# A fused two-block transformer kernel: weight chunks taken later in the delta rule, the last square of each norm summed on TensorE, and a Newton step that needs no square from ScalarE

## What is computed

```
def rms_norm(x, gain):
    xf = x.astype(jnp.float32)
    y = xf * lax.rsqrt(jnp.mean(xf * xf, axis=-1, keepdims=True) + EPS)
    return (y * gain.astype(jnp.float32)).astype(x.dtype)
...
    """Chunked gated delta rule.
    S_t = exp(g_t) (I - beta_t k_t k_t^T) S_{t-1} + beta_t k_t v_t^T,  o_t = S_t^T q_t.
    q, k: [B,H,S,dk] (L2-normed), v: [B,H,S,dv], beta, g: [B,H,S]; float32."""
```

## Time and profile before

| | |
|---|---|
| median of 3 runs | 3218.89 us (3216.57 to 3220.13) |
| profiled execution, its own time | 3218.03 us |
| its span | 3216.2 us |
| granted TensorE clock, mean | 0.955 |
| TensorE busy | 2951.7 us |
| VectorE, ScalarE, GpSimd busy | 1562.7, 1074.6, 195.0 us |

### The profile page before, as it was taken

How to read it: one execution, slowest core, us unless ns; L and a number is a source line. 1 busy time by engine, 2 the same in 40 slices (tenths; PEclk the granted TensorE clock), 3 DMA queues, 4 the chain that set the end, 5 groups by cost and what they waited for, 6 DMA issues and landing times.

```text
span 3216.2 us, 47860 instructions
## 1 busy us (share of the span) xinstructions
PE 2951.7 (92%) x21522; PEld 2380.4 (74%) x21522; DVE 1562.7 (49%) x2201; ACT 1074.6 (33%) x1408; POOL 195.0 (6%) x157
## 2 busy tenths in 40 slices
PE   4999999789999989999799899789999896889999
PEld 3877888567788868888566666578888684578887
DVE  6666554464577643232555555543333655443332
ACT  3225233343233235243422322232222656432221
POOL 1010000201222110001000000010000000000000
PEclk9999999899999989999889888799999998999999
DMA  7554453121000022222110110022323220122321
GB/s 270 183 183 157 183 183 141 53 79 40 16 3 3 17 105 96 101 92 98 56 53 29 39 40 27 14 90 77 115 84 101 77 74 1 51 80 72 118 88 63
DMA packets 41724, 269.66 MB, mean 84 GB/s; under 512 B 4272, under 2 KB 4528, under 8 KB 13488
## 3 DMA queue, kind: packets, MB, share of 16 engines
q1 hardware_dynamic: 39648, 260.86, 22.8%
q10 hardware_dynamic: 1872, 5.74, 0.5%
HBM read 264.49 MB, written 2.10 MB: 83 GB/s over the span
## 4 chain that ended last, share of the span: by engine, by line
PE 81%; DVE 9%; ACT 6%; issue 3%; DMA 1%; POOL 1%; SPq 0%; POOLq 0%; DVEq 0%; ACTq 0%
PE ps L637 19%; PE ps L638 19%; PE ps L643 19%; PE ps L2000 4%; PE ps L2739 1%; PE ps L1578 1%; PE ps L1561 1%; PE ps L1572 1%; PE ps L2058 1%; DVE WL L409 1%; PE ps L2089 1%; DMA W<-w_ada 1%; ACT WH L401 1%; DVE qk L2264 1%; DVE TMP L602 1%
## 5 line engine op out<-in xcount | busy, mean ns | idle before, releaser
L637 PE MATMUL ps<-HH,WH 128*128 128x512 f32 x1928 | 769.3, 399 | 41.3 <-ACT HH L614 39.8
L638 PE MATMUL ps<-HH,WL 128*128 128x512 f32 x1928 | 759.2, 394 | 0.0
L643 PE MATMUL ps<-HL,WH 128*128 128x512 f32 x1928 | 736.6, 394 | 1.0 <-DVE HL L595 1.0
L409 DVE TENSOR_TENSOR WL<-ST,WH 128x2048 fp32r<-128x2048 f32 (+3 forms) x230 | 463.4, 2016 | 266.0 <-ACT WH L401 265.9
L401 ACT ACTIVATE WH<-ST 128x2048 fp32r<-128x2048 f32 (+2 forms) x211 | 382.6, 1813 | 314.5 <-PE ps L643 300.1
L637 PEld LDWEIGHTS ps<-HH,WH 128*128 128x128 f32 x1928 | 368.1, 191 | 130.0 <-issue 51.2
L643 PEld LDWEIGHTS ps<-HL,WH 128*128 128x128 f32 x1928 | 366.7, 190 | 81.4 <-DVE HL L595 3.9
L638 PEld LDWEIGHTS ps<-HH,WL 128*128 128x128 f32 x1928 | 368.1, 191 | 78.7 <-issue 2.9
L637 PE MATMUL ps<-GH,WH 128*128 128x512 f32 x928 | 361.7, 390 | 0.0
L638 PE MATMUL ps<-GH,WL 128*128 128x512 f32 x928 | 361.0, 389 | 0.0
L643 PE MATMUL ps<-GL,WH 128*128 128x512 f32 x928 | 359.8, 389 | 0.0
(11 more groups left out here) (361 smaller groups left out, 3682.3 us busy)
## 6 DMA issues: line engine op xcount, KB each, us to landing
ST<-w_m SPq DMA_DIRECT2D x64, 1024.0 KB, 4.9
ST<-w_gu SPq DMA_DIRECT2D x44, 1024.0 KB, 4.8
ST<-w_ada SPq DMA_DIRECT2D x40, 1024.0 KB, 6.2
ST<-w_dn SPq DMA_DIRECT2D x32, 704.0 KB, 4.1
ST<-w_gin SPq DMA_DIRECT2D x16, 1024.0 KB, 4.7
ST<-w_cin SPq DMA_DIRECT2D x12, 1024.0 KB, 5.0
ST<-w_rkv SPq DMA_DIRECT2D x12, 1024.0 KB, 4.8
ST<-w_kv SPq DMA_DIRECT2D x8, 1024.0 KB, 4.7
```

What stands on the lines that cost most here:

```text
L409: o = e.tensor_tensor(WL[:, j % 3, cut], ST[:, pos % 3, cut], WH[:, j % 3, cut].bitcast(F32), ALU.subtract)
L637: e.matmul(ps[:, :], wh[:, k, cs], H[:, k, :], start=(k == 0), stop=False)
L638: e.matmul(ps[:, :], wl[:, k, cs], H[:, k, :], start=False, stop=False)
L643: o = e.matmul(ps[:, :], wh[:, k, cs], L[:, k, :], start=False, stop=(k == kt - 1))
```

## The change

Three things change.

1. In `tensor_rms`, for all norms of `X` but `final`, GpSimd adds only squares 0 to 6. TensorE multiplies that sum with the ones, and then the eighth square, straight from `TMP`, into the same PSUM tile. The `TMP` buffer of that square is given back by TensorE's step.
2. ScalarE no longer squares the approximate root, anywhere. The Newton step reads the root itself. Its second VectorE instruction was a `tensor_scalar` of one tensor and is now a `scalar_tensor_tensor` of two; its third was a `tensor_tensor` and is now a `scalar_tensor_tensor` of two. In the norms of `X` the `TMP` buffer of the step is now waited for by VectorE.
3. In the delta rule, the chunks of heads 1 to 7 are taken by steps of their own, `take`, at i = 8 and i = 17 of the period before, and the halves of `WL` are at i = 10, 12, 19 and 20, where they were spread over every third position.

```diff
+        def plan_square(tag, k):
+
+            if k == KT - 1 and tag != "final":
+                tmp.use(("square", tag, k), norm_mm, tag)
+            else:
                 tmp.use(("square", tag, k), sumsq, tag, k)
 
...
         def pool_squares(e, tag):
             for k in range(1, KT):
                 for t in squares_of(tag):
+                    if k == KT - 1 and t != "final":
+                        continue
...
         def tensor_rms(e, tag, sums=ACC):
             e.wait_ge(s_tab, 16)
-            e.wait_ge(*sumsq.at(tag, 7))
+            last = tag == "final"
+            e.wait_ge(*sumsq.at(tag, 7 if last else 6))
             e.wait_ge(*sml.free(("rms", tag)))
-            e.matmul(sml.tile(("rms", tag))[:, :], tb("ones"), sums[:, :], start=True,
-                     stop=True).then_inc(*norm_mm.up(tag))
-
-        def scalar_rsqrt(e, into, also, ps, scale, eps, step, *key):
+            o = e.matmul(sml.tile(("rms", tag))[:, :], tb("ones"), sums[:, :], start=True, stop=last)
+            if not last:
+                e.wait_ge(*square.at(tag, 7))
+                o = e.matmul(sml.tile(("rms", tag))[:, :], tb("ones"), tmp.tile(("square", tag, 7)), start=False,
+                             stop=True)
+            o.then_inc(*norm_mm.up(tag))
+
+        def scalar_rsqrt(e, into, ps, scale, eps, step, *key):
 
             n = into.shape[0]
             e.activation(into, ps, ACT.Ln, scale=scale, bias=eps_col(eps)[0:n]).then_inc(*step.up(*key, "ln"))
             e.wait_ge(*step.at(*key, "ln"))
             e.activation(into, into, ACT.Exp, scale=-0.5).then_inc(*step.up(*key, "exp"))
-            e.wait_ge(*step.at(*key, "exp"))
-            e.activation(also, into, ACT.Square).then_inc(*step.up(*key, "sq"))
 
         def vector_rsqrt(e, into, also, ps, scale, eps, step, *key):
 
-            e.scalar_tensor_tensor(out=also, in0=ps, scalar=eps / scale, in1=also, op0=ALU.add,
+            e.scalar_tensor_tensor(out=also, in0=ps, scalar=eps / scale, in1=into, op0=ALU.add,
                                    op1=ALU.mult).then_inc(*step.up(*key, "r"))
             e.wait_ge(*step.at(*key, "r"))
-            e.tensor_scalar(also, also, -0.5 * scale, 1.5, ALU.mult, ALU.add).then_inc(*step.up(*key, "s"))
+            e.scalar_tensor_tensor(out=also, in0=also, scalar=-0.5 * scale, in1=into, op0=ALU.mult,
+                                   op1=ALU.mult).then_inc(*step.up(*key, "s"))
             e.wait_ge(*step.at(*key, "s"))
-            e.tensor_tensor(into, into, also, ALU.mult).then_inc(*step.up(*key, "rstd"))
+            e.scalar_tensor_tensor(out=into, in0=also, scalar=1.5, in1=into, op0=ALU.add,
+                                   op1=ALU.mult).then_inc(*step.up(*key, "rstd"))
 
...
+        def vector_rms(e, tag, eps=1e-6):
+            e.wait_ge(*norm_act.at(tag, "exp"))
...
+        GDN_TAKE, GDN_LOW = (8, 17), (10, 12, 19, 20)
...
-                    if h < 8 and i % 3 == 2:
+                    if h < 7 and i in GDN_TAKE:
+                        out.append(("take", (h + 1, GDN_TAKE.index(i))))
+                    if h < 8 and i in GDN_LOW:
                         out.append(("low", (h, i)))
...
+        def plan_weights(h, n):
+            j = J[f"gin{h}"][n]
+            plan_columns(("take", j))
+            plan_settle(("take", j), len(due))
+            plan_upto(("take", j), j + 2)
+            due.extend((number[sched[pos]], part) for pos in take["take", j] for part in range(2))
+
+        def plan_weights_late(key):
+            plan_weights(*key)
+            yield
+
         def plan_project(h):
             for n, j in enumerate(J[f"gin{h}"]):
-                plan_columns(("take", j))
-                plan_settle(("take", j), len(due))
-                plan_upto(("take", j), j + 2)
-                due.extend((number[sched[pos]], part) for pos in take["take", j] for part in range(2))
+                if h == 0:
...
         def tensor_project(e, h):
             for n, j in enumerate(J[f"gin{h}"]):
-                tensor_columns(e, ("take", j))
+                if h == 0:
+                    tensor_columns(e, ("take", j))
...
+        def tensor_weights(e, key):
+            tensor_columns(e, ("take", J[f"gin{key[0]}"][key[1]]))
+            yield
+
+        def scalar_weights(e, key):
+            scalar_take(e, ("take", J[f"gin{key[0]}"][key[1]]))
+            yield
+
+        def vector_weights(e, key):
+            vector_columns(e, ("take", J[f"gin{key[0]}"][key[1]]))
+            vector_settle(e, ("take", J[f"gin{key[0]}"][key[1]]))
+            yield
...
         def newton(e, into, also, of, *key):
 
-            e.tensor_tensor(also, of, also, ALU.mult).then_inc(*gdn_vec.up(*key, "r"))
+            e.tensor_tensor(also, of, into, ALU.mult).then_inc(*gdn_vec.up(*key, "r"))
             e.wait_ge(*gdn_vec.at(*key, "r"))
-            e.tensor_scalar(also, also, -0.5, 1.5, ALU.mult, ALU.add).then_inc(*gdn_vec.up(*key, "s"))
+            e.scalar_tensor_tensor(out=also, in0=also, scalar=-0.5, in1=into, op0=ALU.mult,
+                                   op1=ALU.mult).then_inc(*gdn_vec.up(*key, "s"))
             e.wait_ge(*gdn_vec.at(*key, "s"))
-            e.tensor_tensor(into, into, also, ALU.mult).then_inc(*gdn_vec.up(*key, "rstd"))
+            e.scalar_tensor_tensor(out=into, in0=also, scalar=1.5, in1=into, op0=ALU.add,
+                                   op1=ALU.mult).then_inc(*gdn_vec.up(*key, "rstd"))
 
```

49 lines of the change are left out of this document (24 added, 25 removed).

## The result

The changed kernel takes 3141.8 us (median of 4 runs, 3135.6 to 3147.1) against 3218.4 us before, a ratio of 0.976 (95% interval 0.974 to 0.978): 76.6 us less. The forecast was 3147 us, 71 us less.

A forecast was written before the change was run, and what follows sets the result against it. TensorE, busy 92% of the span, bounds the kernel, so only its idle time or lower clock can yield. Norms 14.4, delta-rule waits 32.9 and clock 24 give 71 us off 3218.0: 3147 us, range 3120 to 3178.

The forecast's parts named there:

- (a): Norms: the last square goes to TensorE, GpSimd's addition leaves the path and ScalarE's table load ends last; 10.8 us.
- (b): Norms: no square of the root, 0.40 us each, 2.8 us for seven norms, plus 0.8 us elsewhere.
- (c): Delta rule joints, periods 1 to 6: without the chunk L2058 starts 3.45 us earlier, six times; 20.7 us.
- rival C: TensorE does not wait for the chunk; 1.37 us stays at six joints, 3155 us; chance 0.08.
- (d): Delta rule, period 0: the chunk and one half of WL leave the wait of 4.95 us; 3.0 us.
- (e): Delta rule, around the Newton step: a half of WL leaves the chain to L2080 in six periods; 7.3 us.
- (f): Delta rule, output norm: ScalarE's square on 4 columns leaves the chain to L2167, eight times; 1.9 us.
- the forecast's two sums: Delta rule's small Newton step: held beside GpSimd, 3147 us; free of it, about 1.1 us more in eight periods, 3138.
- rival A: The clock gives nothing back, since thin work stands at every joint: 3171 us; chance 0.17.
- B: Rival: the clock gives most back, 50 us, since a period without gaps keeps it up: 3121 us; chance 0.11.
- (g): Delta rule, the chunk's new place and moved halves of WL: counted at nothing, 17 us if cover is gone.
- Rival D: Slower: moved halves of WL delay TensorE and lower its clock, 83 us against 47 gained, 3254 us; chance 0.03.

The follow-up runs named there:

- ten products in the wait: Kernel before, ten useless dense products ahead of TensorE's wait at the joints of periods 1 to 7, chunk unmoved: 3205.9 us.
- filled waits: Useless products ahead of TensorE's waits: kernel before, at joints and the wait for GpSimd, 3188.0 us; changed kernel, whole delta rule, 3127.1 us.
- whole stage filled: Changed kernel with small added products ahead of TensorE's regular waits in the whole delta rule: 3127.1 us.
- halves at once: Changed kernel with the four halves of WL at i = 8, 9, 17 and 18 in place of 10, 12, 19 and 20: 3175.9 us.
- delta rule alone: Kernel before with only the third part of the change, the moved chunks and halves of WL: 3168.0 us.
- mask on VectorE: GpSimd's multiplication moved to VectorE: on the changed kernel 3143.7 us; with the whole delta rule's waits filled, fewer products in one, 3122.0 us.

## Why the prediction was right, and where it was off

**Norms, 14.4 us.** (a) and (b) hold step by step: 1.23 and 0.40 us for each norm were forecast, 8.13 - 6.49 = 1.64 measured, with the table load last, as said, by a margin of only 0.13 us. From the last square to the first dense product the seven norms together gave 13.6 us, which is what (a) and (b) add up to. L556's idle time, 14.0 us in eight cases, is 3.4 in one, the first norm, which is off the path. Outside the delta rule the profiled execution gained 15.8 us.

**Waits in the delta rule, 32.9 us.** The idle time fell by 30.2. (c) held: L2099 waits 0.38 and the state's product not at all, 19.6 us in six periods for the 20.7 forecast, so the chunk was what TensorE waited for, and rival C falls. (d) held: 4.95 us became 2.16 in period 0, 2.8 for 3.0. (e) was too large. The wait for GpSimd's addition fell from 8.6 to 5.7 us in six periods and L2140's 2.1 us went, so 5.0 in place of 7.3. The half of `WL` did leave the chain: from the start of GpSimd's mask to the end of its addition it is 3.81 us in period 3 in place of 4.93. But TensorE got there sooner as well, being at the upper clock on its way, so it waits for more of what is left; I had measured the wait against a slow TensorE. The ten products in the wait show it: in period 3, all at the upper clock and with the half still there, L2140 and L2080 wait 0.6 and 1.4 us, 2.0 in all, and 0.94 is left in the change. (f) held: the eight waits for the output norm fell from 8.6 to 6.6 us, 2.0 for 1.9.

**The rule on contention.** The step in its new form takes 1.27 us beside GpSimd, and 0.16 without it. A `scalar_tensor_tensor` is held just as the `tensor_scalar` was the earlier trace rows. So the forecast was right to count nothing for it. It is this row that decides: the time, 3141.8, lies between the forecast's two sums, 3147 and 3138, and the second was not rightly worked out, since of the wait of 1.43 us only 0.21 was left after (e), and 1.1 could not have come off it. In the Trainium skill this is "SBUF — State Buffer", "Who interferes with whom"; the trace agrees with both of its clauses, on four columns. It agrees with the other direction too: GpSimd's addition is held by VectorE's subtraction that began first, 1.64 for 0.72 us.

**The clock, 24 us.** This is the term that was mis-sized: 34.1 us in the delta rule in the profiled execution, which was 3.9 us under the median of its kernel. The forecast took a value near the lower end of 0 to 64 because thin work stays behind the joint. The filled waits show that this work seldom brings the clock down by itself (once in six periods with the whole stage filled); with idle time beside it, it does so in every period of the kernel before. The periods of 51.1 us are under the 53 to 57 that the forecast gave for them, for this reason. In the profiled execution the sum was 8.8 us too small: 10.1 for the clock and 1.4 outside the delta rule, less 2.7 for the waits. That the median came out only 5 us from the forecast is in part luck. What was right in that argument was period 7: it had no chunk, it kept its idle time and its low clock, 0.83, and gave nothing back. So neither rival A (nothing back) nor B (50 us) came true, and the likeliest case lay between them.

**What was taken at nothing (g).** The halves at i = 10, 12, 19 and 20 cost nothing that shows. That this was a matter of place and not of VectorE's spare time is what the halves at once show, with 34 us. Rival D, a slower kernel, had the right mechanism: a TensorE step delayed by a half of `WL`, and a clock that falls for it. Its price for all four halves, 83 us, was more than twice the 34 that the halves at once cost. It did not come true because the four places chosen here are covered.

## What to carry to other kernels

Where TensorE's granted clock is below 1.00 in a stage, a microsecond of idle time can cost two or three: in the delta rule 30 us of waits taken away gave back 34 us of clock as well (28 and 24 with the delta rule alone), and 13 us of new waits in another order cost 28 us of clock besides. It is no fixed rate: once few waits are left, TensorE's busy time for the same products differs by up to 14 us between executions with the same idle time. Read a wait's price with the busy time of the same products before and after. Before moving work to win such time, a few useless products in the wait tell in one run what the clock alone is worth, and where a wait can't be removed they are a cheap remedy. They are of little use where another engine feeds TensorE no faster than it works, as behind a norm, and can delay a step where they outlast the wait. Put a long VectorE instruction where nothing behind it on its engine, and nothing on GpSimd beside it, is waited for: its place matters more than the share of time in which VectorE is idle.

## What the runs showed that was not expected

- Behind an idle stretch of 0.38 us at a joint, with thin work, the clock falls in some periods and not in others. The changed kernel's four runs spread over 11.5 us, those of the kernel before over 2.8 to 6.4 in its four sets of 4 to 15 runs. With three small products at each joint the spread is 2.7 us.
- With no idle time at all the clock still fell in period 6 of the filled stage.
- A VectorE instruction holds a GpSimd one (1.64 in place of 0.72 us) as a GpSimd one holds VectorE's (1.27 in place of 0.16).
- Small gains did not show alone and did show once the clock was held: the mask on VectorE was worth nothing that can be measured on the changed kernel (3143.7 against 3141.8) and 5.1 us, together with fewer products in one wait, on the one with filled waits.
- The clock behind a norm, which looked like the largest reserve left, gave 0.7 us at one norm and nothing that shows in the time.
